# Diff-attention weight splits on VectorE alone, and eight modulation chunks of the first MLP computed as rows by VectorE in the first mixer

## The reference, cut to what matters

```
# every layer i: six modulation vectors of 1024, for the latent and the context condition
sh_a, sc_a, g_a, sh_m, sc_m, g_m = jnp.split(silu_c @ mod_w[i] + mod_b[i], 6, axis=-1)
h = rms_norm(x, norm_mix_g[i]) * (1 + sc_a) + sh_a
# layer 0: per group of 256 columns a 2-D DFT over tokens and columns, real part, then a projection
y = f @ fourier_w + bias ;  x = x + g_a * y
x = x + g_m * sq_relu_mlp(rms_norm(x, norm_mlp_g[i]) * (1 + sc_m) + sh_m, mlp_w1[i], mlp_w2[i])
# layer 1: 8 heads, two score maps per head, axial rope on the latent half of q and k
p = softmax(s1) - lam * softmax(s2) ;  o = p @ v ;  y = rms_norm(o, subln_g) * (1 - lam_init) @ w_o
```

## Time and profile before

| what | value |
| --- | --- |
| median of 3 runs | 3122.3 us (3122.02 to 3126.4) |
| the profiled execution | 3129.11 us, its span 3127.8 us |
| TensorE, VectorE, ScalarE, GpSimd busy | 97%, 58%, 47%, 36% of the span |
| first mixer, rounds 0 to 8 | about 40 to 116.5 us of the span |
| first mixer, projection with `fw` | 116.5 to 160.0 us |
| differential attention with its `wo` | 520 to 817 us |
| mean granted TensorE clock | 0.992 of 2.4 GHz |

### The profile page before, as it was taken

The page is one execution under the profiler, slowest core; times in us unless marked ns, Lnnn a source line. Parts: engine busy times, 40 slices in busy tenths (PEclk is TensorE's granted clock), DMA queues, the critical chain, the costliest instruction groups (busy, mean ns, idle before and its releaser), DMA issues.

```text
span 3127.8 us, 49696 instructions
## 1 busy us (share of the span) xinstructions
PE 3021.3 (97%) x20396; PEld 2632.8 (84%) x20396; DVE 1809.1 (58%) x3211; ACT 1478.5 (47%) x2501; POOL 1131.2 (36%) x440
## 2 busy tenths in 40 slices
PE   7999999998999999999999999999999999999999
PEld 5878887776788886799999877778999978779999
DVE  2377775566676646577465455654465366654554
ACT  3443333444443324665465446554365456554553
POOL 0322232110323231245455423434555424334554
PEclk9999999999999999999999999999999999999999
DMA  9346652211357632178355433334555433335554
GB/s 309 110 163 199 201 189 95 68 54 32 108 198 253 245 131 73 43 263 270 122 164 186 138 108 95 108 95 140 170 162 170 147 95 109 108 109 162 162 187 137
DMA packets 410705, 459.92 MB, mean 147 GB/s; under 512 B 8688, under 2 KB 389616, under 8 KB 410480
## 3 DMA queue, kind: packets, MB, share of 16 engines
q1 hardware_dynamic: 407392, 453.32, 44.7%
q10 hardware_dynamic: 3088, 3.42, 0.3%
HBM read 455.66 MB, written 1.05 MB: 146 GB/s over the span
## 4 chain that ended last, share of the span: by engine, by line
PE 85%; DVE 9%; ACT 4%; issue 1%; DMA 1%; ACTq 0%; POOL 0%; DVEq 0%
PE bank L434 23%; PE bank L436 23%; PE bank L435 23%; ACT wh L381 2%; DVE wl L397 1%; PE banks L434 1%; PE banks L436 1%; PE banks L435 1%; PE bank L638 1%; DVE bc L2586 1%; PE banks L2549 1%; PE banks L478 1%; PE bank L1424 1%; DMA X<-in_ctxT 1%; PE banks L1770 1%
## 5 line engine op out<-in xcount | busy, mean ns | idle before, releaser
L409 POOL TENSOR_TENSOR wl<-raw,wh 128x768 fp32r<-128x768 f32 (+2 forms) x336 | 1013.4, 3016 | 1826.7 <-ACT wh L381 1826.7
L381 ACT ACTIVATE wh<-raw 128x2048 fp32r<-128x2048 f32 (+1 forms) x336 | 636.0, 1893 | 474.9 <-PE bank L436 407.9
L397 DVE TENSOR_TENSOR wl<-raw,wh 128x1280 fp32r<-128x1280 f32 (+2 forms) x336 | 492.7, 1466 | 506.2 <-ACT wh L381 505.9
L434 PE MATMUL bank<-nh,wh 128*128 128x272 f32 (+1 forms) x1712 | 506.8, 296 | 3.4 <-DVE nl L2134 2.8
L436 PE MATMUL bank<-nh,wl 128*128 128x272 f32 (+1 forms) x1712 | 494.2, 289 | 0.0
L435 PE MATMUL bank<-nl,wh 128*128 128x272 f32 (+1 forms) x1712 | 492.7, 288 | 0.0
L434 PE MATMUL bank<-xh,wh 128*128 128x512 f32 (+2 forms) x1282 | 442.6, 345 | 4.2 <-DVE xl L772 3.7
L436 PE MATMUL bank<-xh,wl 128*128 128x512 f32 (+2 forms) x1282 | 434.9, 339 | 0.0
L435 PE MATMUL bank<-xl,wh 128*128 128x512 f32 (+2 forms) x1282 | 434.8, 339 | 0.0
L434 PE MATMUL bank<-hh,wh 128*128 128x512 f32 (+1 forms) x1024 | 344.1, 336 | 0.0
L435 PE MATMUL bank<-hl,wh 128*128 128x512 f32 (+1 forms) x1024 | 344.1, 336 | 0.0
(11 more groups left out here) (462 smaller groups left out, 5589.9 us busy)
## 6 DMA issues: line engine op xcount, KB each, us to landing
raw<-in_mlp_w SPq DMA_DIRECT2D x128, 1024.0 KB, 5.4
raw<-in_w_in SPq DMA_DIRECT2D x60, 1024.0 KB, 5.3
raw<-in_mod_wT SPq DMA_DIRECT2D x44, 1024.0 KB, 5.1
extra<-in_mod_wT SPq DMA_DIRECT2D x32, 1024.0 KB, 5.3
raw<-in_w_mlp_up SPq DMA_DIRECT2D x32, 1024.0 KB, 5.4
raw<-in_w_mlp_down SPq DMA_DIRECT2D x32, 1024.0 KB, 4.9
raw<-in_w_in SPq DMA_DIRECT2D x34, 512.0 KB, 4.7
raw<-in_w_ssd_down SPq DMA_DIRECT2D x16, 1024.0 KB, 4.9
```

The costliest lines, as they stand in the source:

```text
L381: nc.scalar.activation(self.wtile(self.wh, c1), self.rawtile(c1), AF.Copy).then_inc(*up("act_wh", ("wh", c1)))
L397: nc.vector.tensor_tensor(l, r, h.bitcast(F32), ALU.subtract).then_inc(*up("dve_wl", ("wl_dve", c1)))
L409: nc.gpsimd.tensor_tensor(l, r, h.bitcast(F32), ALU.subtract).then_inc(*up("pool_wl", ("wl_pool", c1)))
L434: nc.tensor.matmul(o, ah, bh, start=first, stop=False)
```

## The change

In the first mixer chunks 12 to 19 of layer 0 become `dmod` chunks, with their own stage name `mix0`. Their 16 halves are placed in VectorE's stream: one each in rounds 5, 6, 7, two in round 8, and 2, 1, 2, 1, 2, 1, 1, 1 ahead of the residuals of the eight groups. TensorE issues four `pe_condition` in rounds 4 and 5; `fa` and `fb` get two banks each, as banks 4 to 7 now hold the conditions. Landing tiles and SyncE's order change with it. In the attention the twelve `qkv` chunks get share 8: VectorE alone makes `wl`, the GpSimd split is skipped, and the split moves from the start of the chunk to behind the beat of half 1 (but for the first chunk). The transposes of finished heads 0 to 4, with `doh` and `dol`, move one beat later.

```diff
                 if L == 0 and j == 0:
-                    mods(0, 8, 20)
+                    mods(0, 8, 12)
+                    dmods(0, 12, 20)
...
-                    w(("qkv", p, j), a["diff_w_qkv"][0], 0, 8, 1024 * i + 256 * j, 256)
+                    w(("qkv", p, j), a["diff_w_qkv"][0], 0, 8, 1024 * i + 256 * j, 256, 8)
...
-        self.extra_first = {extra[0]: (0, 9)}
+        self.extra_first = {extra[0]: (0, 5)}
...
-                t = m % EARLY if m < 2 * EARLY else (2, 5, 6, 7)[m - 2 * EARLY] if m < 20 else 2
+                t = m % EARLY if m < 12 else 2
...
-        self.order = mods[:16] + self.dense[:2] + mods[16:20]
+        dense = self.dense
+        self.order = mods[:13] + dense[:2] + mods[13:14] + dense[2:3] + mods[14:16] + dense[3:4] + mods[16:17] + dense[4:5] + mods[17:18]
+        self.order += dense[5:6] + mods[18:20]
...
+        if L == 0 and i < 20:
+            return "mix0"
...
-            nc.vector.tensor_tensor(l, r, h.bitcast(F32), ALU.subtract).then_inc(*up("dve_wl", ("wl_dve", c1)))
+            nc.vector.tensor_tensor(l, r, h.bitcast(F32), ALU.subtract).then_inc(*up("dve_wl", ("wl_dve", c1), *([("wl_pool", c1)] if n == self.P[c1][2] * self.P[c1][3] else [])))
...
+            if n == self.P[c1][2] * self.P[c1][3]:
+                self.n_pool += 1
+                continue
...
-                    b = self.pe_bank((4, 5) if L == 0 else (4, 5, 6, 7), "fa", L, n, st)
+                    b = self.pe_bank((2, 3) if L == 0 else (4, 5, 6, 7), "fa", L, n, st)
...
-                if n < 8:
+                if n < 4:
                     for i in (2 * n, 2 * n + 1):
                         self.pe_mod(self.ix["mod", 0, i if n < 2 else i + 4])
+                if n in (4, 5):
+                    self.pe_condition("mix0", n - 4, 0)
+                    self.pe_condition("mix0", n - 4, 1)
...
-                    b = self.pe_bank(RING, "fb", L, n - 1, ft)
+                    b = self.pe_bank((0, 1) if L == 0 else RING, "fb", L, n - 1, ft)
...
+                if n >= 5:
+                    self.dve_start_dmods(2 if n == 8 else 1)
         for j in range(4):
             self.dve_split(self.ix["fw", L, j])
             for m in range(2):
                 k = 2 * j + m
+                if L == 0:
+                    self.dve_start_dmods((2, 1, 2, 1, 2, 1, 1, 1)[k])
...
+    def dve_start_dmods(self, n):
+
+        for _ in range(n):
+            i, m = 12 + self.start_dmods // 2, self.start_dmods % 2
+            self.dve_dmod(self.ix["dmod", 0, i], m)
+            self.start_dmods += 1
...
+    def finished(self, s):
+
+        for h in range(8):
+            if s == (9 if h < 5 else 8) + 4 * h:
+                return h
+        return None
...
-        h, b = divmod(s - 8, 4)
-        if b == 0 and 0 <= h < 8:
+        h = self.finished(s)
+        if h is not None:
...
                 c = self.ix["qkv", w, j]
-                self.dve_split(c)
                 if w == "q" and j == 0:
+                    self.dve_split(c)
...
                         self.dve_diff_step(self.beat(w, j, half))
+                        if half == 1:
+                            self.dve_split(c)
```

More of the change, by code:

```diff
@@ L213, in __init__ @@
         extra = [c for c in sorted(self.home) if self.home[c] == EXTRA]
-        self.extra_first = {extra[0]: (0, 9)}
+        self.extra_first = {extra[0]: (0, 5)}
         self.junked = None
-        self.dmod_last = [max(c for c, p in enumerate(self.P) if p[0][0] == "dmod" and self.dmod_stage(c) == st) for st in ("mlp0", "mlp1", "mlp2")]
+        self.dmod_last = [max(c for c, p in enumerate(self.P) if p[0][0] == "dmod" and self.dmod_stage(c) == st) for st in ("mix0", "mlp0", "mlp1", "mlp2")]
         self.dmod_both = max(c for c, p in enumerate(self.P) if p[0][0] == "dmod" and self.dmod_conditions(c) == 2)
@@ L221, in __init__ @@
         self.turning = self.adding = None
-        self.nmod = 0
+        self.nmod = self.start_dmods = 0
         self.hid = {}
@@ L319, in homes @@
             last[t] = c
-        self.order = mods[:16] + self.dense[:2] + mods[16:20]
+        dense = self.dense
+        self.order = mods[:13] + dense[:2] + mods[13:14] + dense[2:3] + mods[14:16] + dense[3:4] + mods[16:17] + dense[4:5] + mods[17:18]
+        self.order += dense[5:6] + mods[18:20]
         late = mods[20:]
         for d, c in enumerate(self.dense):
-            if d < 2:
+            if d < 6:
                 continue
@@ L1141, in act_fourier @@
                 self.act_fourier_high(L, 2 * n + 1, 1)
-            if L == 0 and n < 8:
+            if L == 0 and n < 4:
                 self.act_mod(self.ix["mod", 0, (2 * n if n < 2 else 2 * n + 4) + 1])
```

## The result

The changed kernel takes **3112.3 us** (median of 6 runs, 3111.8 to 3115.6), the one before 3123.8 us beside it (6 runs, 3122.0 to 3127.2): ratio 0.9964 (95% interval 0.9952 to 0.9977, in brackets from here on), 11.6 us less. The prediction said 12.8 less, from 3122.3 to 3109.5, and 3100 to 3121. The profiled execution took 3112.4 us, its span 3111.1.

What follows compares the result with a forecast made beforehand. TensorE, busy 97% of the span, was taken as the bound. Attention -18.6 and first mixer +5.8 gave -12.8 us, 3129.1 to 3116.3 for the profiled execution; put on the median, 3122.3 to 3109.5, range 3100 to 3121.

Steps and rivals of the forecast that it cites:

- Mixer, TensorE and queue: First mixer: TensorE saves 5.4 us, but VectorE's 45.1 us queue of halves and residuals swallows it; 1.8 us lost.
- within 0.1 us: First mixer, rounds 5 to 8: two banks each for `fa` and `fb` cost nothing, the tightest place coming out within 0.1 us.
- rival (c): First mixer: late loads into two landing buffers stop VectorE, 49 us, total +36, 3158 us; chance 0.06.
- The worse end of this term: First mixer, VectorE's queue: a loss of 6 us if two loads take 8.3 us, not 5.4.
- Mixer, clock: Head of `mlp0`: some eight idle us of TensorE lower its clock, costing 4 us, between zero and 6.8.
- The estimate of 3.4 us: Head of `mlp0`: by the Trainium skill's rule, half of 6.8 us of low clock is lost, instead of 4.
- Attention: Attention stage: stalls and rope waits 13.5 and clock 6.8 gained, less 1.0 and 0.7: 18.6 us faster.
- Stalls: Attention: three projection stalls for `dpt` (7.6 us) and five rope waits for `tmp` (5.9) go, 13.5 us.
- three new waits of 0.35 us: Attention: one new wait of 0.35 us per period, as ScalarE copies `dq` only behind the exp; 1.0 us in all.
- They vanish doubly: Attention: the `tmp` waits (5.9 us) go by the moved split, and also since five `dx` move one beat later.
- GpSimd out of the splits: Attention, 12 of 16 chunks: removes the 1.3 us blocked rope in a stall; the split's place accounts for 1.4.
- Clock: Attention: two 20 us windows averaging 0.83 recover, 3.4 us each, 6.8 us; clock stays at 1.00 until 745 us.

Runs made afterwards that it cites:

- e7: Changed kernel with VectorE's context instruction in the mixer's sixteen halves cut to a one-column `tensor_scalar` (output differs): 3101.0 us, ratio 0.9922.
- e6: Changed kernel plus 13 useless 256-column matmuls at the head of `mlp0`, where TensorE idles: 3109.7 us, ratio 0.9946.
- e5: Changed kernel with the finished heads transposed at s = 8 + 4h again, as before the change: 3116.0 us, ratio 0.9968.
- e9: Kernel before with only VectorE's split of `qkv` chunks moved behind the second beat; GpSimd share, heads and mixer old: 3112.7 us, ratio 0.9967.
- e4: Changed kernel with VectorE and GpSimd sharing the `qkv` splits 5 to 3 as before, the split still moved: 3111.4 us, ratio 0.9953.
- e1: Kernel before with only the attention part of the change, the first mixer as before: 3107.9 us, ratio 0.9942.
- e3: Changed kernel with share 8 kept but VectorE's split left at the start of each `qkv` chunk: 3118.4 us, ratio 0.9976.
- e11: Repeat run: attention part, with only four mixer chunks instead of eight by VectorE as rows: 3105.3 us, ratio 0.9941.
- e2: Kernel before with only the mixer part of the change, the attention as before: 3131.2 us, ratio 1.0017.
- e10: Repeat run of the kernel with only the attention part, the first mixer as before: 3107.5 us, ratio 0.9953.

## Why the prediction was right, and where it was not

**The forecast held**: both signs, both stages, and the sum to 1.2 us (11.6 for 12.8). But part of that is luck: the clock gave 3.2 us less in the attention than reckoned and cost 1.8 us less in the mixer, the waits gave 1.0 us more, and 1.3 us are open, so errors of both signs cancel.

**Mixer, TensorE and queue: right.** Against the turn, the splits of round 8 end 5.9 us earlier (reckoned 5.4). In e7, whose halves take VectorE half as long, it is 6.4, so TensorE saves 1 us more than reckoned, and some 0.5 us of it is lost in the rounds; I had written within 0.1, and TensorE's timeline has one new wait of 0.35 us for `al`. The queue behind them took 45.6 us (159.70 - 114.11; reckoned 45.1). Within it one block more by GpSimd than I counted, three of 1.2 us instead of two, and 0.3 us for the load instead of 0.7. The last residual is 1.9 us later than before, counted from the turn; reckoned 1.8. The loads of these chunks landed in 5.3 to 5.9 us at the median (one of `fw` in 7.5) and held VectorE for 0.3 us; rival (c) did not come about, though e7 shows that the loads are not far behind. The worse end of this term, a loss of 6 us with two loads at 8.3, is about 1 us too high by my own slacks of 4.8 and 7.8 us. By the DMA issues, 100 to 165 us:

```profile
raw<-in_mod_wT SPq DMA_DIRECT2D x4, 1024.0 KB, 5.9
...
extra<-in_mod_wT SPq DMA_DIRECT2D x3, 1024.0 KB, 5.3
```

**Mixer, clock: right in kind, too large.** I took 4 us between 0 and 6.8. It was 2.0 to 2.2 (e6), so the mixer lost 4.25 instead of 5.8: 1.9 up to the last residual and 2.4 behind it, of which the last 0.4 are open. The idle time was as reckoned, 7.9 us for some 8; what I had too large is how much work the low clock would lengthen: it was little more than the conditions, by 2.3 us. The estimate of 3.4 us, from the Trainium skill, *TensorE: Matmul & The Clock Gate*, section "HAM oscillation", was nearer. But its rule, half of the throttled time, applied to the low clock of this trace, gives an estimate of 5.2 us: by the two windows behind the projection it was at its half level for 7.5 and 2.9 us (twice one minus the clock, times the length). The measurement decides for 2.0 to 2.2; by windows of 2 us TensorE had no work in some 3.5 of the 10.2 us at the low level.

**Attention: the sum right, the causes partly wrong.** Reckoned -18.6, measured -17.7.
- Stalls: 13.5 to go, 1.7 new. The waits between 580 and 760 us fell by 12.8 (19.9 to 7.1). Of the three new waits of 0.35 us two appear, 1.0 us together.
- "They vanish doubly", of the waits for `tmp`: wrong. Without the moved heads 3.1 of the 5.9 us remain (e5), and in e9 2.2. The move of the heads is worth 2.8 to 3.5 us (e5 against the changed kernel, e9 against e4, whose mixers differ but not their attention otherwise), a term that I had set at nothing.
- GpSimd out of the splits: I split the stall into 1.4 for the place of the split and 1.3 for the blocked rope. e9 bears that out: with the place alone 1.3 of the 2.87 us go and 1.55 stay. But I gave the second part to GpSimd's leaving, and e4 shows that the moved heads remove it as well. By the stage, taking GpSimd out makes no difference over 0.1 us with the moved heads (e1 against e4) and brings 0.4 without them (e5 against e9): there it spares two stalls of 0.5 and 1.5 us, but the waits for `tmp` are 0.9 us longer (the split takes 0.8 us more) and the late stalls 2.4 us. e9 has 14.5 of the 17.7 us without touching the share.
- Clock: -6.8 reckoned. By the windows, one minus the clock times 20 us, the two that averaged 0.83 lost 6.8 and are clean; a new low of 2.0 + 3.0 us stands at 720 to 760, where I wrote that the clock would stay at 1.00 until 745 us and that the late stalls would leave it alone, because they had the earlier trace rows. The stage of before had another 0.91 from 800 to 820 (1.8 us), which is gone too. Net -3.6. It does not come with the stalls alone: e3 and e5, with longer waits in all, have no such fall, the changed kernel, e1, e4 and e6 to e11 do. Why, I can't say.
- 12.8 and 3.6 make 16.4; the remaining 1.3 us I can't assign.

**The medians** give 11.6 where the stages give 13.4. The traced execution of before, 3129.1 us, was longer than all six timed ones, and e2 shows 2.8 us more in a stage of the same code, with more lost clock. That its falls were unfavourable is likely, but I have no second trace of that kernel to show it. The timed runs of both kernels fall into two groups (last section): 3122.0 to 3122.4 and 3125.2 to 3127.2 before, 3111.8 to 3112.4 and 3115.1 to 3115.6 after. Lower against lower the change gives 10.3 us, upper against upper 11.1, so the 13.4 of the two traces are at the favourable end.

## What to carry to other kernels

In a stream written out by hand, the place of one instruction can matter more than its length: a split 0.8 us longer in a slack place beat a short one ahead of a dependent chain, and the share between the engines was worth 0.4 us at most there. Look also at what stands ahead of the chain: `dol` moved behind the rope let the rope finish before GpSimd's split began. Work moved from a full engine to an idle one pays only while the idle engine's whole queue, blocks by its neighbours included, ends ahead of the full one; eight chunks gave 45.6 us of queue and lost 4, four chunks left slack and won 1.4. Split a change of several parts before judging it: here one part lost a quarter of what the other had won.

## What was not expected of the hardware

**The start has two courses.** TensorE has the same work in all kernels up to the turn in round 4, yet that turn starts at 74.9 to 76.4 us in ten of the traces and at 78.7 to 79.0 in three (before, e2, e5). It is not the change: e9 and e10 have the old mixer and start early, e2 has the new one and starts late. The timed runs fall into two groups about as far apart (3111.8 to 3112.4 and 3115.1 to 3115.6 for the changed kernel), which fits but is not shown to be the same thing, as they left no traces. TensorE's timeline before, at the start:

```profile
33.70 1.84 PE L1005 MATMUL banks<-ones,rs 128*128 128x1 f32 x8
...
42.40 0.63 PE L435 MATMUL banks<-tl,xh 128*128 128x512 f32 x1
...
49.31 0.40 PE L435 MATMUL banks<-tl,xh 128*128 128x512 f32 x1
```

and in the changed kernel:

```profile
33.43 1.03 PE L1013 MATMUL banks<-ones,rs 128*128 128x1 f32 x8
...
42.26 0.63 PE L443 MATMUL bank<-tl,xh 128*128 128x512 f32 x1
43.28 0.40 PE L443 MATMUL bank<-tl,xh 128*128 128x512 f32 x1
```

Eight small matmuls take 1.84 us in the one and 1.03 in the other. The 128x512 matmuls follow each other at 0.43 us (1.2 GHz), later at 0.23 us; the slow ones last until 46.7 us in the one and until 42.7 in the other. So TensorE ran at 1.2 GHz up to 46.7 us in three traces. In the ten others it was at full clock from about 32 to 35 or 36 us, fell again (the windows of the changed kernel show 0.50 from 38 to 42) and was back at full clock between 42 and 45. The granted clock of the windows does not tell all of this: the kernel before has 1.00 at the slow matmuls,

```profile
42.00:44.00 2.00, 2.00 (x5) 1.61 (x6) 1.73 (x11) 1.88 (x5) 0.00 (x0) 1.00 1.10 348
```

so at the start durations have to be read instead. Whoever compares two traces takes marks behind the start and compares differences.

**Busy work can pay.** 13 matmuls of 256 columns without a use (26 in the trace's count), in time that was idle anyway, made the first mixer 2.2 us shorter (e6).
